# Four key projections taken apart and put between the score tiles of differential attention

## The reference, cut to what matters

```python
proj = h @ w_in                      # 512 x 6960: q_da k_da v_da | q_ns | kc vc ks vs kw vw | gates
y_da = diff_attention(q_da, k_da, v_da, ...)     # 8 heads, two softmaxes each, causal
y_ns = nsa(q_ns, kc_raw, vc_raw, ks_raw, vs_raw, kw_raw, vw_raw, g_ns, ...)

def diff_attention(q, k, v, ...):    # per block of 128 queries and head
    p = softmax(q @ k.T * scale + causal)        # two of them, c = 0 and 1
    a = p[:, :, 0] - lam * p[:, :, 1]
    o = rmsnorm(a @ v, head_gain) * (1.0 - lam_init)

def compress(x_raw, pos, w1, w2):    # kc_raw and vc_raw: blocks of 32 tokens, stride 16
    return gelu((blocks(x_raw) + pos) @ w1) @ w2

ks, kw = apply_rope(k_slc), apply_rope(k_win)    # ks_raw and kw_raw are rotated
```

## Time and profile before

| | us |
|---|---|
| median of 3 runs | 2101.65 (2101.18 to 2110.67) |
| the profiled execution | 2101.01 |
| its span, from the first to the last instruction | 2099.2 |

### The profile page before, as it was taken

The page is one execution under the profiler, slowest core; times in us unless marked ns, Lnnn a source line. Parts: engine busy times, 40 slices in busy tenths (PEclk is TensorE's granted clock), DMA queues, the critical chain, the costliest instruction groups (busy, mean ns, idle before and its releaser), DMA issues.

```text
span 2099.2 us, 25667 instructions
## 1 busy us (share of the span) xinstructions
PE 2016.0 (96%) x10244; PEld 1696.5 (81%) x10244; DVE 1042.3 (50%) x1606; ACT 814.6 (39%) x1482; POOL 276.5 (13%) x272
## 2 busy tenths in 40 slices
PE   6999999999999999999998899989899999999998
PEld 6887888888888888888887688777777888888887
DVE  5675565555353222335545766766565543222333
ACT  5442443333343222324225744455554333222322
POOL 1001000000000000000012432376763000000000
PEclk9999999999999999999998999999999999999999
DMA  5231233333223333332541043212115423332332
GB/s 192 81 101 61 100 102 101 92 99 101 92 90 102 99 100 92 99 101 81 151 130 41 1 171 120 90 31 61 46 37 180 126 80 105 96 101 92 99 100 71
DMA packets 58982, 200.13 MB, mean 95 GB/s; under 512 B 8080, under 2 KB 8112, under 8 KB 58480
## 3 DMA queue, kind: packets, MB, share of 16 engines
q1 hardware_dynamic: 53936, 178.29, 27.1%
q0 software_dynamic: 4928, 20.21, 2.7%
HBM read 181.16 MB, written 8.39 MB: 90 GB/s over the span
## 4 chain that ended last, share of the span: by engine, by line
PE 76%; DVE 7%; POOL 5%; ACT 5%; issue 3%; DVEq 2%; DMA 1%; POOLq 1%; SPq 0%; ACTq 0%
PE ps L636 24%; PE ps L637 24%; PE ps L638 24%; POOL PU L592 5%; DMA raw<-in_w_all 1%; DVE Wl L1703 1%; DVE XN L1743 1%; PE ps L1089 1%; DVEq L2262 1%; POOLq L581 1%; PE ps L1005 1%; ACT Pb L1371 1%; ACT Wh L1210 1%; DVE AUl L2267 1%; ACT PL L1466 1%
## 5 line engine op out<-in xcount | busy, mean ns | idle before, releaser
L1703 DVE TENSOR_TENSOR Wl<-raw,Wh 128x1024 fp32r<-128x1024 f32 x307 | 378.3, 1235 | 754.1 <-ACT Wh L1210 752.7
L636 PE MATMUL ps<-HTh,Wh 128*128 128x512 f32 (+1 forms) x1728 | 647.4, 375 | 8.9 <-DVE HTl L1752 7.0
L638 PE MATMUL ps<-HTh,Wl 128*128 128x512 f32 (+1 forms) x1728 | 641.9, 371 | 0.0
L637 PE MATMUL ps<-HTl,Wh 128*128 128x512 f32 (+1 forms) x1728 | 641.6, 371 | 0.0
L1210 ACT CAST Wh<-raw 128x1024 fp32r<-128x1024 f32 x307 | 322.0, 1051 | 782.5 <-DMA raw<-in_w_all 782.5
L636 PEld LDWEIGHTS ps<-HTh,Wh 128*128 128x128 f32 x1728 | 327.5, 190 | 64.7 <-issue 9.7
L638 PEld LDWEIGHTS ps<-HTh,Wl 128*128 128x128 f32 x1728 | 327.0, 189 | 56.1
L637 PEld LDWEIGHTS ps<-HTl,Wh 128*128 128x128 f32 x1728 | 327.3, 189 | 54.0
L636 PE MATMUL ps<-Wh,Yh 128*128 128x512 f32 x528 | 205.8, 390 | 0.0
L638 PE MATMUL ps<-Wh,Yl 128*128 128x512 f32 x528 | 205.5, 389 | 0.0
L637 PE MATMUL ps<-Wl,Yh 128*128 128x512 f32 x528 | 205.4, 389 | 0.0
(11 more groups left out here) (281 smaller groups left out, 2370.0 us busy)
## 6 DMA issues: line engine op xcount, KB each, us to landing
raw<-in_w_all SPq DMA_DIRECT2D x307, 512.0 KB, 3.5
swp_d<-qkd SPq DMA_DIRECT2D x64, 64.0 KB, 2.7
g_dram<-gst SPq DMA_DIRECT2D x16, 256.0 KB, 4.0
ring<-g_dram POOLq DMA_DIRECT2D x16, 256.0 KB, 3.5
gpre<-in_g_pre POOLq DMA_DIRECT2D x5, 512.0 KB, 3.8
X<-in_x SPq DMA_DIRECT2D x4, 512.0 KB, 5.0
swp_r<-qkr SPq DMA_DIRECT2D x16, 128.0 KB, 2.3
cw1k<-in_cw POOLq DMA_DIRECT2D x1, 2048.0 KB, 8.6
```

What stands on the lines that cost most here:

```text
L636: tensor.matmul(dst, a_hi, b_hi, start=start, stop=False)
L637: tensor.matmul(dst, a_hi, b_lo, start=False, stop=False)
L638: return tensor.matmul(dst, a_lo, b_hi, start=False, stop=stop)
L1703: vector.tensor_tensor(Wl[:, s, :], raw[:, s, :], Wh[:, s, :], ALU.subtract).then_inc(w_lo, 1)
```

## The change

It does four things.

1. The 32 products of `nsf` (4 chunks of 8 blocks of the inner dimension) become steps of three matmuls, `nsf_steps`. Six run after the first two score tiles, one after each `turn` of tiles 0 to 25. They accumulate in bank 7, so the values of attention keep bank 6 alone. ScalarE copies a finished chunk out (`nsf_out`) at the start of tiles 2, 10, 18 and 26 and splits the next weights at the end of them; VectorE does its half at the end of the same tiles.
2. Raw keys go where query and key tiles are dead (`kraw`, `swp_n`, `kcv`), and other tiles get new addresses. The first-half compression weights `cw1k` load once the last low part is made; the second set of additions comes before `YD` is written out.
3. The squares of `YD` are taken in two halves, into two free places, with the splits of `nst` between the parts; the normalisation of `YD` follows the key rotations and the low parts of the values.
4. The high and low parts of the rotated keys (`ksh`, `ksl`) move from query chunks 0 and 1 to 4 and 5, and TensorE waits for `ks_lo` before the first scores of `nsa`.

```diff
-    ("nsf", 4, [1, 1, 1, 1, 0, 0, 0, 0], [0] * 8),
+    ("nsf", 4, [0, 0, 0, 0, 0, 0, 0, 4], [0] * 8),
+    ("da", 0, [0] * 8, [16, 16, 16, 16, 16, 16, 32, 0]),
     ("nst", 3, [1, 1, 1, 1, 0, 0, 0, 0], [0] * 8),
...
-        DSQ = at("DSQ", 64, [P, TT, D])
+        DSQ = [at("DSQ0", 0, [P, 2, D]), at("DSQ1", 76, [P, 2, D])]
         cw1k = at("cw1k", 16, [P, 16, 256])
         cw1v = at("cw1v", 48, [P, 16, 256])
...
-        kcv = at("kcv", 64, [P, 2, SEQ])
+        kcv = at("kcv", 88, [P, 2, SEQ])
...
-        kraw = at("kraw", 44, [P, 2, SEQ])
+        hid4 = at("hid4", 65, [P, 2, 2, 4, 32])
+        kraw = at("kraw", 8, [P, 2, SEQ])
...
-        swp_n = at("swp_n", 76, [P, 2, SEQ])
+        swp_n = at("swp_n", 12, [P, 2, SEQ])
...
+        FIRST_STEPS = 6
+        def nsf_ends(t):
+            done = FIRST_STEPS + t
+            return done // 8 - 1 if done % 8 == 0 and 8 <= done <= 32 else None
...
-                c = m - CHUNK0["nsf"]
-                if c in (2, 3) and on("nsf"):
-                    swap("nsf", c - 2, c, 0, kraw[:, c - 2, :], swp_n[:, c - 2, :])
+                if m == CHUNK0["nsf"] + 3 and on("nsf"):
+                    for c in range(2):
+                        swap("nsf", c, 7, 2 + c, kraw[:, c, :], swp_n[:, c, :])
...
                 v_low(0, 7)
-                for b in (6, 7):
-                    pl.wait_ge(full[b], FILLED["nsf"][b])
+                if on("cmp"):
+                    pool.drain()
+                    load(posT[:], t["posT"], in_pos)
+                    load(cw1k[:].rearrange("p j n -> p (j n)"), t["cw1"][0], in_cw)
+                pl.wait_ge(full[6], FILLED["da"][6] + TOTAL)
                 load(cos[:], t["c_cos_n"], in_rope)
                 load(sin[:], t["c_sin_n"], in_rope)
...
-                for tt in range(TT):
-                    pl.wait_ge(da_fin, tt + 1)
-                    pl.dma_start(y_dram[tt], YD[:, tt, :]).then_inc(yd_out, 16)
                 def inputs(kv):
...
-                    pl.wait_ge(free[kv], FREED["nst"][kv])
+                    pl.wait_ge(free[7], FREED["nsf"][7] + kv + 1)
...
                 inputs(0)
+                load(w2k[:], t["w2k"], in_cw)
+                load(w2v[:], t["w2v"], in_cw)
+                inputs(1)
+                pool.drain()
+                for tt in range(TT):
+                    pl.wait_ge(da_fin, tt + 1)
+                    pl.dma_start(y_dram[tt], YD[:, tt, :]).then_inc(yd_out, 16)
                 pl.wait_ge(yd_out, 16 * TT)
                 load(cw1v[:].rearrange("p j n -> p (j n)"), t["cw1"][1], in_cwv)
-                inputs(1)
-                pool.drain()
...
-                b = 6 + u
-                bank_free("da", b, t // 2)
+                b = 6
+                bank_free("da", b, t)
...
+            def nsf_steps(a, b):
+                for n in range(a, b):
+                    c, k = n // 8, n % 8
+                    w = weights(CHUNK0["nsf"] + c)
+                    if k == 0:
+                        bank_free("nsf", 7, c)
+                    q = slice(k * P, (k + 1) * P)
+                    last = three(ps[7][:], Wh[:, w, q], Wl[:, w, q], HTh[:, k, :], HTl[:, k, :], k == 0, k == KT - 1)
+                    if k == KT - 1:
+                        last.then_inc(w_used, 1)
             def attention():
                 scores(0)
                 scores(1)
+                nsf_steps(0, FIRST_STEPS)
                 for t in range(TOTAL):
                     if exists(t - 2):
                         values(t - 2)
                     if exists(t + 2):
                         scores(t + 2)
                     turn(t)
+                    if FIRST_STEPS + t < 32:
+                        nsf_steps(FIRST_STEPS + t, FIRST_STEPS + t + 1)
...
-                for b in range(8):
-                    pe.wait_ge(free[b], FREED["da"][b])
                 pe.wait_ge(st_zero, 1)
                 attention()
-            if on("nsf"):
-                for c in range(4):
-                    gemm_f("nsf", c, c)
...
+                pe.wait_ge(ks_lo, 1)
...
+                filled("da", 6, t)
+                scalar.activation(YD[:, t % 4, span(0, 2 * P, t // 4 * P, P)], ps[6][:, 0:P], ACT.Copy,
+                                  scale=rr[:, t % STEPS, 0:1]).then_inc(free[6], 1)
+            def nsf_out(c):
+                chunk_done("nsf", c)
+                if c >= 2:
+                    ac.wait_ge(st_lo, 4 * (4, 7)[c - 2] + 2)
+                dst = kcv[:, c, :] if c < 2 else kraw[:, c - 2, :]
+                scalar.copy(dst, ps[7][:]).then_inc(free[7], 1)
             def attention():
                 exps(0)
+                high_parts(0, 0, 1)
                 exps(1)
+                high_parts(0, 1, 0)
                 for t in range(TOTAL):
-                    if exists(t - 3):
-                        da_out(t - 3)
+                    if nsf_ends(t) is not None:
+                        nsf_out(nsf_ends(t))
+                    if exists(t - 2):
+                        da_out(t - 2)
                     high(t)
                     if t % 4 == 1 and exists(t + 4):
                         high_parts(0, t // 4 + 1, 1)
...
                         high_parts(0, t // 4 + 2, 0)
                     if exists(t + 2):
                         exps(t + 2)
-                for t in range(TOTAL - 3, TOTAL):
-                    da_out(t)
+                    if nsf_ends(t) is not None:
+                        split(CHUNK0["nsf"] + nsf_ends(t) + LEAD)
...
+                    if head == 0:
+                        ac.wait_ge(free[6], FREED["da"][6])
...
-                scalar.activation(DSQ[:], YD[:], ACT.Square).then_inc(da_sq, 1)
-                ac.wait_ge(da_ss, 1)
+                for n in range(2):
+                    scalar.activation(DSQ[n][:], YD[:, 2 * n:2 * n + 2, :], ACT.Square).then_inc(da_sq, 1)
+                split(CHUNK0["nst"] + LEAD)
+                ac.wait_ge(da_ss, 2)
                 scalar.activation(hsd[:], hss[:], ACT.Sqrt, scale=1.0 / P, bias=eps[:]).then_inc(da_sd, 1)
-                for c in range(4):
-                    split(CHUNK0["nsf"] + c + LEAD)
-                    chunk_done("nsf", c)
-                    dst = kcv[:, c, :] if c < 2 else kraw[:, c - 2, :]
-                    scalar.copy(dst, ps[c][:]).then_inc(free[c], 1)
             if on("nst"):
-                for c in range(3):
-                    split(CHUNK0["nst"] + c + LEAD)
+                split(CHUNK0["nst"] + 1 + LEAD)
...
+                split(CHUNK0["nst"] + 2 + LEAD)
...
-                    if c == 0:
+                    if c == 4:
+                        ac.wait_ge(cm_a, 2)
...
+                    if nsf_ends(t) is not None:
+                        split(CHUNK0["nsf"] + nsf_ends(t) + LEAD)
...
-                ve.wait_ge(da_sq, 1)
-                vector.tensor_reduce(hss[:], DSQ[:].rearrange("p i (h d) -> p (i h) d", d=P), AX.X, ALU.add).then_inc(da_ss, 1)
-                ve.wait_ge(da_sd, 1)
-                vector.reciprocal(hrs[:], hsd[:])
-                vector.drain()
-                for i in range(TT):
-                    r = hrs[:, i * 8:(i + 1) * 8].rearrange("p (h a) -> p h a", a=1).broadcast_to((P, 8, P))
-                    blk = YD[:, i, :].rearrange("p (h d) -> p h d", d=P)
-                    vector.tensor_tensor(blk, blk, r, ALU.mult).then_inc(da_fin, 1)
-                for c in range(4):
-                    split(CHUNK0["nsf"] + c + LEAD)
+                for n in range(2):
+                    ve.wait_ge(da_sq, n + 1)
+                    vector.tensor_reduce(hss[:, 16 * n:16 * n + 16], DSQ[n][:].rearrange("p i (h d) -> p (i h) d", d=P), AX.X,
+                                         ALU.add).then_inc(da_ss, 1)
+                split(CHUNK0["nst"] + LEAD)
...
                 keys_out(0)
-                split(CHUNK0["nst"] + LEAD)
+                ve.wait_ge(da_sd, 1)
+                vector.reciprocal(hrs[:], hsd[:])
+                vector.drain()
                 split(CHUNK0["nst"] + 1 + LEAD)
                 keys_out(1)
...
+                split(CHUNK0["nst"] + 2 + LEAD)
+                for i in range(TT):
+                    r = hrs[:, i * 8:(i + 1) * 8].rearrange("p (h a) -> p h a", a=1).broadcast_to((P, 8, P))
+                    blk = YD[:, i, :].rearrange("p (h d) -> p h d", d=P)
+                    vector.tensor_tensor(blk, blk, r, ALU.mult).then_inc(da_fin, 1)
...
-                    if c == 1:
+                    if c == 3:
+                        cmp_shift(0)
+                    if c == 5:
                         ve.wait_ge(ks_hi, 1)
                         vector.tensor_tensor(ksl[:].rearrange("p a g n -> p (a g n)"), ksw[:].rearrange("p a g n -> p (a g n)"),
-                                             ksh[:].rearrange("p a g n -> p (a g n)"), ALU.subtract)
+                                             ksh[:].rearrange("p a g n -> p (a g n)"), ALU.subtract).then_inc(ks_lo, 1)
```

28 lines of the change are left out of this document (7 added, 21 removed).

## The result

The changed kernel takes 2116.35 us, median of 12 runs (2112.81 to 2123.23), against 2102.98 of before (12 runs, 2100.86 to 2110.67): ratio 1.006, 95% interval 1.0045 to 1.0075. It is slower; 2094.1 was forecast. The profiled execution took 2117.22, its span is 2115.4, 16.2 more than before.

A forecast was written before the change was run, and what follows sets the result against it. TensorE, busy 96% of the span, was taken as the bound. Attention's 14.2 us gain, less 6.5 for clock and 0.2 behind attention, took 7.5 off 2101.01: 2093.5, or 2094.1 as median; own range 2090 to 2098, wider 2083 to 2101.

The forecast's parts named there:

- Start: Before attention's first scores: the wait for all eight banks goes, leaving a pause of 1.0 us instead of 3.4.
- Splits inside attention: At tiles 2, 10, 18, 26: TensorE waits behind VectorE's subtraction, 2.4 us three times and 3.2 once, 10.5 in all.
- Sum at full clock: Attention with key projections, pauses included, before clock falls: 110.8 us against 125.0, so 14.2 us less.
- Clock: Half-clock stretches after three of the four split pauses in attention: 6.5 us lost in all, bounds 0 and 13.6.
- Behind attention and `ksl`: Moved squares, `YD` normalisation and `ksl` after attention: mostly hidden, cost between 0 and 2.3 us, taken as 0.2.
- Queues: DMA and GpSimd order behind attention: `cw1v` lands at 45 us, needed at 47.3; two us of slack, cost 0.
- The rival on the slower side: At the second compression matmul: `cw1v` comes late, TensorE waits 8.7 us, 2102.8 us in all; chance 0.08.

The follow-up runs named there:

- e3: The changed kernel without the read of `cw1v`, the second compression matmul using the first one's weights instead: 2102.61 us, ratio 0.9995 to the kernel before.
- e1: The changed kernel with ScalarE's copy of the queries ahead of its weight-chunk cast at query chunk 3: 2107.34 us, ratio 1.0015 to the kernel before.

## Why the prediction was wrong

- *Start:* 1.0 forecast, 1.23 measured. Right.
- *Splits inside attention:* 2.4 three times and 3.2 forecast, 2.40, 2.15, 2.14 and 2.63 measured, at the instruction named and for the reason named; taking the subtraction out of the way took them away. Right.
- *Sum at full clock:* 110.8 forecast. Measured 124.8; less the clock's 12.2 at most, 112.6 or a little more. Right in size, partly by luck, since two errors nearly cancel: without the pauses I would have said 100.3, and the run without them took 106.0, so the rest was 5.7 too low; and taking the pauses out gave 6.6, not 10.5. Waits of 0.73 us for the copy out of the one bank 7, which I had not seen, the pause of 1.24 us in the first head and the edges of the stage make up the difference.
- *Clock:* 6.5 forecast, at most 12.2 measured. The mechanism was right for the pauses at the splits, the term mis-sized. I took 2.5 us a fall, between two rows; three of the four pauses had one, each of the long kind (7.0 us, against 6.8 after the 1.89 us pause of the earlier trace rows), which cost at most 3.5, 3.5 and 2.6. And I gave the last head nothing of its own, where a fall behind its pause of 1.33 us cost 2.6 more up to the first `nst` matmul. Of the 7.5 us by which attention missed, 5.7 are this term's and 1.8 the sum's. I had also put a pause of 3.35 us without a fall on the other side, and not seen that the pause of 3.38 us in the earlier trace rows had 6.8 us at half clock with it: part of what attention took before was clock as well. The table in the Trainium skill ("TensorE: Matmul & The Clock Gate", "Why this matters for your kernels") warns only of idle gaps longer than these; the falls at 2.15 to 2.63 us say otherwise.
- *Behind attention and `ksl`:* 0.2 forecast. With both causes out, the stretch took 82.62 against 82.54 before. Right.
- *Queues:* this is the step that failed and made the change slower. I followed `cw1v` to its own reader ("two us of slack; cost 0"), and there I was close: it landed 47.2 us after the first `nst` matmul (1279.92 and 10.1, less 1242.81), 45 forecast, and no one waited for it, though of the two us of slack nothing was left (47.3 was the demand). I did not ask what else was in the DMA engines in those 10 us, nor how much slack that had: the weight chunk had half a us, since its cast ends at 1288.46 and the query copy behind it starts at 1288.97. Cost: a pause of 4.45 us instead of 0.69, and up to 11.7 us of clock, most of the 16.9; taking the transfer out (e3) or the cast out of the copy's way (e1) gave it back.
- *The rival on the slower side* had `cw1v` late by 8.7 us of GpSimd's idling ahead of each set of additions. It idled 3.53 and 2.44 behind small loads; the long idle times (8.67, 8.15 and 10.94 us) all stand behind 2 MB. Right transfer, wrong victim.

The error in sum: 7.5 us in attention (124.8 against 117.3) and 16.7 behind it, less 0.6 outside, are, to rounding, the 23.7 by which the profiled execution missed 2093.5.

## What to carry to other kernels

When a large transfer moves, list what else is in the DMA engines while it runs, and for each its reader, the queue in which that reader stands, and what is behind it there. A cast for a chunk needed five chunks later must not stand ahead of a copy that TensorE needs next. A pause is worth its length and the half clock that follows, and ahead of a long run of narrow matmuls the second part was here up to three times the first.
